# Norm roots computed as columns and spread by the tensor engine, in a two-block transformer kernel on one core

## The reference

```python
def rms_norm(x, g):                         # norms of both blocks
    y = x * lax.rsqrt(jnp.mean(x * x, axis=-1, keepdims=True) + NORM_EPS)
    return y * g
# layer l of the first block
h = rms_norm(x, norm_g[l]) * (1 + scale) + shift      # then h @ w_in[l]
...
# end of the second block
x = x + rms_norm(y @ w_out, post_mix_norm)            # tag "mo"
f = ffn(rms_norm(x, pre_ffn_norm))                    # w_up, convolution, gelu gate, w_down
x = x + rms_norm(f, post_ffn_norm)                    # tag "fo"
e = (p @ w_ple) * sigmoid(x @ w_ple_gate)             # w_ple, w_pg
out = x + rms_norm(e, ple_norm)                       # tag "em"
```

## Time and profile before

| | |
|---|---|
| median of the runs | 3246.94 us |
| the profiled execution | 3253.76 us, span 3252.0 us |
| PE matmul busy | 2995.8 us (92%), weight load 2768.1 us |
| DVE busy | 2265.5 us (70%) |
| ACT busy | 1624.1 us (50%) |
| POOL busy | 334.0 us (10%) |
| mean DMA | 177 GB/s, SP's queue 49.1% of 16 engines |

### The profile page before, as it was taken

How to read it: one execution, slowest core, us unless ns; L and a number is a source line. 1 busy time by engine, 2 the same in 40 slices (tenths; PEclk the granted TensorE clock), 3 DMA queues, 4 the chain that set the end, 5 groups by cost and what they waited for, 6 DMA issues and landing times.

```text
span 3252.0 us, 60643 instructions
## 1 busy us (share of the span) xinstructions
PE 2995.8 (92%) x24264; PEld 2768.1 (85%) x24264; DVE 2265.5 (70%) x3538; ACT 1624.1 (50%) x2409; POOL 334.0 (10%) x587
## 2 busy tenths in 40 slices
PE   6889989998988799999899999999799999999987
PEld 2677777887977789999798889989799999999987
DVE  6367777588788877775666566666688845887565
ACT  3335655355565554745334342545555544555454
POOL 0012322100123131300000000110100000000000
PEclk8899999998999899999999998999899999999989
DMA  9877766874645346555233333555355555555543
GB/s 372 290 241 239 242 207 214 282 276 138 184 134 155 103 151 204 177 175 171 91 102 106 101 112 100 166 159 187 127 172 184 183 188 177 185 184 169 187 145 115
DMA packets 168745, 577.01 MB, mean 177 GB/s; under 512 B 39760, under 2 KB 39792, under 8 KB 156048
## 3 DMA queue, kind: packets, MB, share of 16 engines
q1 hardware_dynamic: 146784, 525.40, 49.1%
q0 software_dynamic: 21104, 44.27, 4.6%
q10 hardware_dynamic: 576, 3.47, 0.3%
HBM read 546.83 MB, written 17.83 MB: 174 GB/s over the span
## 4 chain that ended last, share of the span: by engine, by line
PE 59%; DVE 25%; ACT 8%; DMA 4%; issue 3%; SPq 1%; DVEq 0%; ACTq 0%; POOL 0%
PE acc L950 58%; DVE arena L910 7%; DVE rounded L910 6%; ACT arena L947 4%; DVE arena L920 3%; ACT rounded L947 2%; DVE upper L910 2%; DVE upper L920 1%; ACT L947 1%; ACT upper L947 1%; DVE rounded L920 1%; PE acc L953 1%; SPq L906 1%; DMA arena<-in_w_ada 1%; DMA arena<-in_w_in 1%
## 5 line engine op out<-in xcount | busy, mean ns | idle before, releaser
L950 PE MATMUL acc<-rounded 128*128 128x256 f32 x14688 | 1941.2, 292 | 52.9 <-issue 30.3
L950 PEld LDWEIGHTS acc<-rounded 128*128 128x128 f32 x14688 | 1845.3, 196 | 137.8 <-issue 103.8
L910 DVE TENSOR_TENSOR rounded<-arena,rounded 128x1024 fp32r<-128x1024 f32 (+1 forms) x832 | 1003.9, 1207 | 311.7 <-ACT rounded L947 242.8
L947 ACT ACTIVATE rounded<-arena 128x1024 fp32r<-128x1024 f32 (+1 forms) x864 | 883.8, 1023 | 648.7 <-PE acc L950 449.1
L950 PEld LDWEIGHTS acc<-upper_rounded,rounded 128*128 128x128 f32 x4560 | 553.2, 193 | 25.8 <-issue 14.2
L950 PE MATMUL acc<-upper_rounded,rounded 128*128 128x256 f32 x4560 | 560.8, 285 | 9.6 <-DVE rounded L910 5.5
L947 ACT ACTIVATE arena<-arena 128x256 f32<-128x256 f32 (+4 forms) x477 | 252.9, 530 | 308.5 <-DVE arena L910 207.3
L950 PE MATMUL acc<-arena 128*32 128x512 f32 (+5 forms) x1622 | 250.3, 480 | 59.8 <-DVE arena L910 22.8
L910 DVE TENSOR_TENSOR arena<-arena 128x256 f32<-128x256 f32 (+5 forms) x471 | 258.6, 549 | 49.9 <-ACT arena L947 30.1
L910 DVE TENSOR_TENSOR arena<-acc,arena 128x256 f32<-128x256 f32 (+3 forms) x280 | 119.0, 425 | 204.0 <-PE acc L950 181.1
L920 DVE SCALAR_TENSOR_TENSOR arena<-arena 128x256 f32<-128x256 f32 (+5 forms) x461 | 205.6, 446 | 59.2 <-ACT arena L947 31.2
(11 more groups left out here) (91 smaller groups left out, 1194.3 us busy)
## 6 DMA issues: line engine op xcount, KB each, us to landing
arena<-in_w_in SPq DMA_DIRECT2D x328, 512.0 KB, 4.5
arena<-in_w_ada SPq DMA_DIRECT2D x88, 1024.0 KB, 5.2
arena<-in_w_up SPq DMA_DIRECT2D x176, 512.0 KB, 4.1
arena<-in_w_down SPq DMA_DIRECT2D x88, 512.0 KB, 4.1
arena<-in_w_outa SPq DMA_DIRECT2D x32, 512.0 KB, 6.0
arena<-in_w_glu SPq DMA_DIRECT2D x32, 512.0 KB, 6.2
arena<-in_w_outm SPq DMA_DIRECT2D x32, 512.0 KB, 4.6
arena<-in_w_out SPq DMA_DIRECT2D x32, 512.0 KB, 4.3
```

The source lines that it names most:

```text
L910: return self.put(self.e and self.e.tensor_tensor(o, a, b, op))
L947: return self.put(self.e and self.e.activation(o, a, f, scale=scale, **kw))
L950: return self.put(self.e and self.e.matmul(o, l, r, start=start, stop=stop, skip_group_check=True))
```

## The change

Five edits:

1. For "mo", "fo", "em" and ("x", 0) PE makes the sums of squares as two columns (128x2, tokens on the partitions), ACT takes the root of 128x2 into the new `NCOL`, DVE inverts 128x2, and PE spreads the result over all partitions by two products with the unit matrix (`recip` of PE). The scaling reads the roots from PSUM bank 3. The first norm ("x0") and `rmsf` stay as they were.
2. A new beat `warm`, one Sqrt of 128x1 on ACT, behind the first matmuls of the last tile of `w_outm` (both layers), `w_out2` and `w_down1`. No such beat stands in `w_pg`.
3. `post` is split in `scale` and `post`. The order becomes scale 0, post 0, scale 1, low halves of group 0, post 1, scale 2, low halves of group 1, and so on.
4. The squares at "mo" are added by DVE (`sum4`), as background steps behind blocks 15, 23 and 31 of `w_up`, not by POOL.
5. `w_pg` leaves `PAIRS`. Its first 64 blocks go over output tiles 0 to 3 with four inputs each: k = 0..3 of the four tiles, then k = 4..7, and so on. Its weights are packed in that order.

```diff
@@ _c = Cursor(N1)
-QR, QI = _c.alloc(64), _c.alloc(64)
+QR, QI, NCOL = _c.alloc(64), _c.alloc(64), _c.alloc(4)
-PAIRS = (("w_in", 48), ("w_in2", 0), ("w_up", 0), ("w_pg", 0))
+PAIRS = (("w_in", 48), ("w_in2", 0), ("w_up", 0))
+QUADS = (("w_pg", 0),)
@@ class Timeline, def stream
+            quads = (name, u0) in QUADS
+            if quads and blk < 64:
+                n, k = n0 + blk // 4 % 4, 4 * (blk // 16) + blk % 4
             self.add("mm", t, k, p, blk % 8)
+            if (name, n, k) in (("w_outm", 15, 0), ("w_out2", 15, 0), ("w_down1", 15, 0)):
+                self.add("warm")
+    def scaled(self, tag, g):
+        if g == 0:
+            self.add("scale", tag, 0)
+        self.add("post", tag, g)
+        if g < 3:
+            self.add("scale", tag, g + 1)
+
+    def square_sums(self):
+        yield
+        for g in range(1, 4):
+            self.add("sum4", g)
+            yield
@@ def run
-        for g in range(5):
-            if g < 4:
-                self.add("post", "mo", g)
-            if g:
-                for k in range(4 * g - 4, 4 * g):
-                    self.add("hf", k)
-                self.add("sqf", g - 1)
+        for g in range(4):
+            self.scaled("mo", g)
+            for k in range(4 * g, 4 * g + 4):
+                self.add("hf", k)
+            self.add("sqf", g)
         self.add("ff_first")
+        self.bgs.append(self.square_sums())
@@
-        for g in range(5):
-            if g < 4:
-                self.add("post", "fo", g)
-            if g:
-                self.add("xs", g - 1)
+        for g in range(4):
+            self.scaled("fo", g)
+            self.add("xs", g)
@@
         for g in range(4):
+            self.add("scale", "em", g)
             self.add("post", "em", g)
@@ def tensor_program
     def rms(tag, total):
-        pe.mm(B(3, 0, 256), con("ones"), V(RS2, 256), True, True).then_inc("norm_pe", tag)
+        for th in range(2):
+            x = pe.mm(B(3, th, 1), V(RS2 + 128 * th, 128), con("ones", 1), True, True)
+        x.then_inc("norm_pe", tag)
+
+    def recip(tag):
+        if tag in ("x0", "hf"):
+            return
+        pe.wait_ge("norm_dve", ("col", tag))
+        for th in range(2):
+            x = pe.mm(B(3, 128 * th, 128), V(NCOL + th, (0, 128)), con("ident"), True, True)
+        x.then_inc("norm_pe", ("over", tag))

     def rmsf():
-        pe.wait_ge("sum_pool", ("hf", 3))
+        pe.wait_ge("sum_dve", ("hf", 3))
+        pe.wait_ge("x_dve", ("mo", 3))
@@ s5_run, b == 0
-                pe.wait_ge("norm_act", ("sqrt", ("x", 0) if l else "x0"))
+                if l:
+                    pe.wait_ge("rhs", ("h", 1, 15))
+                else:
+                    pe.wait_ge("norm_act", ("sqrt", "x0"))
@@ def scalar_program
     def rms(tag, total):
         act.wait_ge("norm_pe", tag)
-        act.act(V(RS, 256), B(3, 0, 256), ACT.Sqrt, bias=con("eps"), scale=1.0 / 2048).then_inc("norm_act", ("sqrt", tag))
+        if total is None:
+            to, sums = V(RS, 256), B(3, 0, 256)
+        else:
+            to, sums = V(NCOL, 2), B(3, 0, 2)
+        act.act(to, sums, ACT.Sqrt, bias=con("eps"), scale=1.0 / 2048).then_inc("norm_act", ("sqrt", tag))
+
+    def warm():
+        act.act(V(NCOL + 2, 1), con("eps"), ACT.Sqrt)
@@ def vector_program
     def recip(tag):
         dve.wait_ge("norm_act", ("sqrt", tag))
-        dve.recip(V(RS, 256), V(RS, 256))
+        if tag in ("x0", "hf"):
+            dve.recip(V(RS, 256), V(RS, 256))
+        else:
+            dve.recip(V(NCOL, 2), V(NCOL, 2)).then_inc("norm_dve", ("col", tag))
@@ def h
+            if l:
+                dve.wait_ge("norm_pe", ("over", ("x", 0)))
+            root = B(3, 0, 256) if l else V(RS, 256)
-            dve.stt(V(UT + 256 * j, 256), V(X + 256 * j, 256), V(GP + j, 1), V(RS, 256), MUL, MUL).then_inc("h_dve", (l, j))
+            dve.stt(V(UT + 256 * j, 256), V(X + 256 * j, 256), V(GP + j, 1), root, MUL, MUL).then_inc("h_dve", (l, j))
@@
+    def sum4(g):
+        dve.wait_ge("norm_act", ("sqf", g))
+        dve.tt(V(AR, 1024), V(AR, 1024), V(AR + 1024 * g, 1024), ADD).then_inc("sum_dve", ("hf", g))
+
+    def scale(tag, g):
+        t = V(src + 1024 * g, 4, 256)
+        dve.wait_ge(sem, ("ev", tl.out_of[stream, 0, 4 * g + 3].o))
+        dve.wait_ge("norm_pe", ("over", tag))
+        dve.tt(t, t, B(3, 0, (0, 4), (1, 256)), MUL)
+
     def post(tag, g):
-        dve.wait_ge(sem, ("ev", tl.out_of[stream, 0, 4 * g + 3].o))
-        dve.tt(t, t, V(RS, (0, 4), (1, 256)), MUL)
         dve.tt(x, x, V(src + 1024 * g, 1024), ADD).then_inc("x_dve", (tag, g))
@@ def gpsimd_program
-    def sqf(g):
-        pool.wait_ge("norm_act", ("sqf", g))
-        if g:
-            pool.tt(V(AR, 1024), V(AR, 1024), V(AR + 1024 * g, 1024), ADD).then_inc("sum_pool", ("hf", g))
@@
+def pack_quads(W):
+    b = W[:, :512].reshape(4, 4, 128, 4, 128).transpose(0, 2, 3, 1, 4)
+    return np.concatenate([b.reshape(4, 128, 2048), pack(W[:, 512:])])
-    A["w_pg"] = pack(g["w_ple_gate_2"][0])
+    A["w_pg"] = pack_quads(g["w_ple_gate_2"][0])
```

More of the change, by code:

```diff
@@ L100 @@
 HALF = 1024
-N1, N2 = 25348, 11392
+N1, N2 = 25348, 11400
 NF = NS * 2 * HALF + 2 * 4096
@@ L464, in stream @@
             n, k = n0 + at // nk, at % nk
-            if at % 16 == 0 and not ((name, u0) in PAIRS and blk < 16):
+            quads = (name, u0) in QUADS
+            if quads and blk < 64:
+                n, k = n0 + blk // 4 % 4, 4 * (blk // 16) + blk % 4
+            if at % 16 == 0 and not ((name, u0) in PAIRS and blk < 16) and not (quads and blk < 32):
                 self.want(name, u0 + at // 16)
@@ L483, in stream @@
                 held.append(t)
-            if late is not None and blk == 39:
+            if late is not None and blk == (71 if quads else 39):
                 late()
@@ L1400, in mla @@
             pe.mm(B(5, 128, 128), v1, V(MPT + 256, 128), False, True).then_inc("mla_pe", ("o", h))
-    play = dict(mm=mm, ev=ev, mod=mod, modend=modend, sq=sq, rms=rms, rms2=rms2, rmsf=rmsf, lam=lam, s5_prep=s5_prep, s5_run=s5_run, att=att,
+    play = dict(mm=mm, ev=ev, mod=mod, modend=modend, sq=sq, rms=rms, recip=recip, rms2=rms2, rmsf=rmsf, lam=lam, s5_prep=s5_prep, s5_run=s5_run, att=att,
                 rw=rw, rw_seq=rw_seq, rw_post=rw_post, kk=kk, cq_norm=cq_norm, mla=mla)
@@ L1791, in ev @@
             act.act(V(EM + 256 * n, 256), V(EM + 256 * n, 256), ACT.Copy, scale=par("ple_norm", n)).then_inc("g_act", key)
-    play = dict(begin=begin, hi=hi, modrow=modrow, sq=sq, rms=rms, rms2=rms2, rmsf=rmsf, h=h, hf=hf, sqf=sqf, xs=xs, lam=lam, tables=tables, part=part,
+    play = dict(begin=begin, hi=hi, modrow=modrow, sq=sq, rms=rms, warm=warm, rms2=rms2, rmsf=rmsf, h=h, hf=hf, sqf=sqf, xs=xs, lam=lam, tables=tables, part=part,
                 s5_setup=s5_setup, s5_prep=s5_prep, s5_sine=s5_sine, s5_run=s5_run, s5_out=s5_out, att=att, rw_first=rw_first, rw=rw,
@@ L2245, in mla @@
             dve.ts(V(MPR + 128, 256), V(MPR + 128, 256), V(MSM + 3, 1), None, MUL).then_inc("mla_dve", ("w", h))
+    def sum4(g):
+        dve.wait_ge("norm_act", ("sqf", g))
+        dve.tt(V(AR, 1024), V(AR, 1024), V(AR + 1024 * g, 1024), ADD).then_inc("sum_dve", ("hf", g))
+    def scale(tag, g):
+        src, stream, sem = {"mo": (MO, "w_out2", "ev_act"), "fo": (FO, "w_down1", "g_act"), "em": (EM, "w_pg", "g_act")}[tag]
+        t = V(src + 1024 * g, 4, 256)
+        dve.wait_ge(sem, ("ev", tl.out_of[stream, 0, 4 * g + 3].o))
+        dve.wait_ge("norm_pe", ("over", tag))
+        dve.tt(t, t, B(3, 0, (0, 4), (1, 256)), MUL)
     def post(tag, g):
-        src, stream, sem = {"mo": (MO, "w_out2", "ev_act"), "fo": (FO, "w_down1", "g_act"), "em": (EM, "w_pg", "g_act")}[tag]
-        t, x = V(src + 1024 * g, 4, 256), V(X + 1024 * g, 1024)
-        dve.wait_ge(sem, ("ev", tl.out_of[stream, 0, 4 * g + 3].o))
-        dve.tt(t, t, V(RS, (0, 4), (1, 256)), MUL)
+        src, x = {"mo": MO, "fo": FO, "em": EM}[tag], V(X + 1024 * g, 1024)
         dve.tt(x, x, V(src + 1024 * g, 1024), ADD).then_inc("x_dve", (tag, g))
@@ L2376, in vector_program @@
                 rw_zero=rw_zero, rw_first=rw_first, rw=rw, kkn=kkn, rw_seq=rw_seq, rw_post=rw_post, rw_std=rw_std, cq_norm=cq_norm, cq=cq,
-                mla=mla, post=post, ev=ev)
+                mla=mla, sum4=sum4, scale=scale, post=post, ev=ev)
     for beat, *of in tl.beats:
@@ L2493, in gate @@
             gates[0] += 1
-    def sqf(g):
-        pool.wait_ge("norm_act", ("sqf", g))
-        if g:
-            if g > 1:
-                pool.wait_ge("sum_pool", ("hf", g - 1))
-            pool.tt(V(AR, 1024), V(AR, 1024), V(AR + 1024 * g, 1024), ADD).then_inc("sum_pool", ("hf", g))
     def ff_first():
@@ L2546, in gpsimd_program @@
     play = dict(begin=begin, pos2=pos2, s5_setup=s5_setup, s5_first=s5_first, s5_prep=s5_prep, s5_y=s5_y, s5_yr=s5_yr, att=att, rw_first=rw_first,
-                rw=rw, extras=extras, cq_load=cq_load, sqf=sqf, ff_first=ff_first, ev=ev)
```

(4 more changed lines are left out.)

## The result

The changed kernel takes 3242.93 us, median of 15 runs (3232.45 to 3248.53), beside 3253.77 us for the kernel before, also 15 runs (3244.66 to 3264.74). The ratio is 0.9966, with a 95% interval of 0.9953 to 0.9978: 11 us faster, 7 to 15. The forecast was 3236.4 with a range of 3233 to 3242.5, so the time lies 0.4 us above its range, though the sum of the gains, 10.6 us, was near 10.8, the difference of the two medians. The three runs of before that were known ahead (3246.94, 3246.91, 3251.76) were on the low side of the fifteen.

The account below looks back on a forecast made before the run. PE held 59% and DVE 25% of the chain, and only the joints between matrices could move. Terms 7.1 + 3.9 + 1.1 - 0.1 - 1.45 = 10.6 us, taken from 3246.94, gave 3236.4 us, 80% range 3233 to 3242.5.

Parts of the forecast that it names:

- The base: Whole kernel: the time the gain is subtracted from, 3246.94 us by median, 6.8 us below the profiled execution's 3253.76.
- "mo": 7.1 forecast: At "mo": earlier first scaling (1.5 us) and no POOL sums on DVE's path start `rmsf` 7.1 us earlier.
- "fo": 3.9 forecast: At "fo" and in `w_pg`: DVE's low half of weight 773 sets PE's restart; 3.9 us gained.
- "em": 1.1 forecast: At "em": roots in columns shorten the chain to the first scaling, without `warm`; 1.1 us gained.
- "x" 0: 0.1 lost forecast: At norm "x" 0: an extra table load and root cost 1.55 us, a shorter chain returns about 1.45.
- Layer 1: 1.45 lost forecast: In layer 1: `warm` adds a load and root on ACT, which has no slack; 1.45 us lost.
- "w_up": 0 forecast: Between `rmsf` and the sum at "fo": no change, 0 us.
- A clock that holds the low level through the joints: At "mo" and "fo": PE stays at its low clock, leaving 1.2 us gain, 3245.8 us; chance 0.08.
- The second rival: At "mo": POOL is not what stretches the low halves, so 6.05 us stay, 3242.4 us; chance 0.05.
- The slower case: Scalings at "mo", "fo", "em": fourfold PSUM reads take twice as long, adding 15 us, 3251.4 us; chance 0.04.
- The fourth rival: Its place, claim and size are left out of the text given; chance 0.10.
- The fifth: In `w_up` and `w_pg`: transfers or emptying set the pace and the gain is given back, about 3246 us; chance 0.03.

Follow-up runs that it names:

- experiment 11: The changed kernel, with no further edit, run and profiled again; median 3243.80 us.
- experiment 5: The changed kernel with the old order of scaling and low halves at "mo" and "fo"; median 3240.97 us.
- experiment 2: The kernel before with only the squares at "mo" moved from POOL to DVE; median 3248.08 us.
- experiment 1: The changed kernel with the squares at "mo" added by POOL again; median 3249.07 us.
- experiment 7: The changed kernel with idle matmuls ahead of the spreading, two at "mo" and "fo", three at "em"; median 3242.66 us.
- experiment 9: The kernel before with only the roots in columns, spread by PE, and scaling from PSUM; median 3248.89 us.
- experiment 4: The changed kernel with `w_pg` beginning in pairs again instead of quarters; median 3244.34 us.
- experiment 3: The changed kernel without the `warm` beats, so without the early table load; median 3240.42 us.
- experiment 10: The changed kernel without `warm` in `w_outm`, with the old order of scaling and low halves and two idle matmuls at "mo"; median 3238.40 us.

## Why the prediction was off, point by point
**The base: the step that failed.** The working gave two numbers, 3243.2 from the profiled execution and 3236.4 from the median of three, and I took the second ("The median of the runs lies 6.8 us below that execution, and I subtract from it"). The first is 0.3 us from the measured 3242.93. A median of three executions that spread over 5 us, with the profiled one 6.8 above, isn't a base known to 0.1 us: in the fifteen, single executions of before spread over 20 us (3244.66 to 3264.74), and their median is 3253.77. The spread was in sight at the prediction, and the range held only doubts about the terms and none about the base. That the sum of the gains came so near is in part luck: "mo" fell 1.8 us short, "fo" and "em" 0.4 each, layer 1 lost 0.15 more, and "w_up", put at nothing, gave 1.6 the other way. By the joints 9.4 us are gained, and the rest of the 10.8 lies in stretches that scatter by 12.

**"mo": 7.1 forecast, 5.35 measured.** The mechanism holds: without POOL's additions the lows take 2.25 and 4.03 us, and `rmsf` waits for `sum4` (0.61 us measured, 0.5 forecast). Two terms were mis-sized. The spreading took 1.22 and not 0.65 us, since the clock fell just as it began; so the first scaling gained 0.8 and not 1.5. In experiment 11, where it took 0.71, the joint gained 5.85. And `rmsf` starts 28.5 us after the first scaling (2348.50 - 2319.96), not 27.4. Of these 1.1 us 0.65 lie in the four groups: the last low half ends 20.5 us behind the first scaling (2338.21 + 2.25 - 2319.96) and not 19.85. The interleaving, which I had counted as 0.2 gained, costs 0.8: in experiment 5 `rmsf` starts 27.7 us after the first scaling. The other 0.5 lie behind the groups, where low halves and `sum4` start 1.33 us apart and I had put 1.25 to 1.27.

**"fo": 3.9 forecast, 3.47 measured,** and the place of the wait was right. DVE set the point 17.95 us after the first scaling (3139.00 - 3121.05), where I had 17.6; PE's 74 matmuls took 11.17 us, where I had 12.2 for 72, since the clock was high again earlier, from 3131.0. In part the agreement is luck, because before's 109.43 is itself the worse of two outcomes: it ran at the low clock until 3144.9. Against the 107.15 of the same code in experiment 2, the gain is 1.2. The changed kernel had 105.9 in four profiles (after, experiments 1, 7, 11). Edit 1 has 1.6 of it (experiment 9), measured against that same 109.43; the quarters have 0.5 at most by experiment 4.

**"em": 1.1 forecast, 0.66 measured.** Again the spreading at the low clock, 1.18 instead of 0.65 us; in experiment 11, where it took 0.71, the gain was 1.1.

**"x" 0: 0.1 lost forecast, 0.05 measured,** as two sizes that cancel: columns give 1.6, the thrown-out table costs 1.6 (experiment 3).

**Layer 1: 1.45 lost forecast, 1.60 measured,** which is the load and the root, 1.28 + 0.30, with the gap between: at 1361.31 + 1.28 = 1362.59 the load is over, and the root starts at 1362.61. Experiment 3 gives back 1.6.

**"w_up": 0 forecast, 1.56 measured.** This isn't in any term. It is also not steady: the same kernel gained only 0.6 in experiment 11. Part is a wait of PE at the border of `w_up` and the matrix behind it, before and after:
```profile
2604.70 15.49 PE L950 MATMUL acc<-upper_rounded,rounded 128*128 128x256 f32 x127 [1.33 <-DVE rounded L910]
```
```profile
2591.97 28.22 PE L969 MATMUL acc<-upper_rounded,rounded 128*128 128x256 f32 x232
```
The wait is in before (1.33 us) and in experiment 2 (0.93), and in none of the eleven profiles with edit 1. Experiment 9 has edit 1 alone and no wait, so neither the order nor the sums nor the quarters are needed to take it away. Why edit 1, which issues nothing there, does so is open.

**The rivals.** A clock that holds the low level through the joints (3245.8) is not what happened: at "fo" it was high after some 21 matmuls (0.76 in 3130 to 3132, so from about 3131, and PE began at 3126.28: 4.7 us by 0.22), in the kernel before after some 36. But a fallen clock is what made the gains at "mo" and "em" smaller: I had looked for it only behind the joint, and it sat in the spreading too. The second rival, that POOL doesn't stretch the low halves, has the price nearest to the measured time (3242.4 beside 3242.93), but only because its base was too low as well: experiments 1 and 2 refute it. The slower case, a dear fourfold read of PSUM, is refuted: 1.22 us a scaling, against the 2.15 from which it would decide. The forecast had the 1.22 right by a slope that its rows don't give: between 954 ns for 768 columns and 1267 for 1024 lie 1.22 ns a column and not 1.04. The 1.04 is the slope of the PSUM form by itself: 954 ns for 768 columns before, 1221 for 1024 in after. The PSUM operand cost nothing that shows, 1.22 us beside 1.22 to 1.23 for SBUF. The fourth rival has 0.10 of the chances and a part in the range; no run shows a table load that costs more than its own 1.28 us (in "x" 0 and in layer 1 the next activation starts 0.01 to 0.02 us behind it), and ACT's delay in layer 1 cost no more than the one wait (1.60 us). The fifth, that the gain is given back within `w_up` or `w_pg`, isn't seen: "w_up" and "fo" both got shorter.

**What each edit is worth,** by joints: roots in columns 6.1 us (experiment 9, 0.7 of it the open "w_up"); squares off POOL 5.0 in the old order, 3.5 in the new; quarters 0.5; the early load -2.9 by "x", layer 1 and "mo", -1.3 by all joints; the interleaving -1.1 by all joints, -1.9 by "mo" and "fo" alone (experiment 5). These add up to 5.3 to 9.2 us where 9.4 were measured; each was taken once, with other edits around it and with its own outcome of the clock, and the rest is not assigned. With the early load of `w_outm` and the interleaving left out, and two idle matmuls at "mo", the kernel is faster than with all five, by 4.4 us of the joints (experiment 10).

## What to carry to other kernels
Take the base of a forecast from as many executions as there are, and put its scatter into the range: here it was larger than the error of the sum of all terms. A small product in a wait of PE must be costed at both levels of the clock: at "mo" the spreading took 0.99 us or more in six of the eleven profiles that have it, and 0.71 in five, three of them with idle matmuls. Before an early table load is added, look at what that engine does between the load and its use: here a Sin between them had the Sqrt table loaded again (loads at 772.18, 773.85 and 778.24), and in layer 1, where ACT had no slack, the load cost its whole length, 1.28 of the 1.60 us.

## What the runs showed of the hardware
- **PE's clock at short stops is not the same in every execution.** The spreading at "mo" of one kernel took 1.22 us in one profile and 0.71 in the other; behind one wait of 1.56 us 108 matmuls took 13.21 us, so 0.122 each, and within 3 us behind one of 1.89 the clock was at 0.50. What decides between them is not worked out here. Two idle matmuls ahead of the spreading went with a later fall at "mo" and "fo" (4.7 to 6.0 us after the sum's start, 1.6 to 4.0 without), and did not hold it at "em" in one of two kernels.
- **Beside an addition of POOL a DVE addition took 2.07 us longer.** One of 128x1024 took 3.30 us instead of 1.23 when POOL's of 2.44 had started 0.2 us earlier. So taking POOL's three additions over, at 3.7 us of DVE's own time, freed the joint by 3.5 to 5 us.
- **A table load took 1.28 us and nothing besides** (1283 ns on average over the 54 of after). In the rows above where the next activation waits for nothing else, it starts 0.01 to 0.02 us after it.
- **Scaling with a repeated PSUM operand** (each column four times) took 1.22 us, as additions of the same size with both operands in SBUF did.
